# Attention scores of 96 rows as two 128-row passes and a block of four 32-row products

## The reference

```
s = (einsum('bqhd,bkhd->bhqk', qn_b, k_nope)
     + einsum('bqhr,bkr->bhqk', qr_b, k_rope)) * scale
p = softmax(s, axis=-1)
out = einsum('bhqk,bkhd->bqhd', p, v)
```

## Time and profile before

| | |
|---|---|
| median of 3 runs | 634.62 us (634.34 to 634.89) |
| profiled execution, its time | 635.12 us |
| its span in the trace | 633.3 us |
| PE / DVE / ACT / POOL busy | 99% / 69% / 56% / 50% of the span |
| PE idle before its last work | under 3 us in all |
| last matmul to the end | some 6 us |

### The profile page before, as it was taken

One profiled execution on the slowest core, in us unless ns is written; L12 is line 12 of the kernel. 1 busy time (PEld: TensorE's weight loads), 2 busy tenths in 40 slices (PEclk: granted clock), 3 DMA queues, 4 the chain that ended last, 5 costly groups with the idle time before them and its releaser, 6 DMA issues.

```text
span 633.3 us, 9322 instructions
## 1 busy us (share of the span) xinstructions
PE 624.8 (99%) x3253; PEld 525.8 (83%) x3253; DVE 439.2 (69%) x852; ACT 355.6 (56%) x765; POOL 316.4 (50%) x302
## 2 busy tenths in 40 slices
PE   8999999999999999999999999999999999999996
PEld 7889888888888887888887888888888888888885
DVE  4773335334434349999998788888888888799694
ACT  6652223213333237777776777777777778542563
POOL 3634004405656433543635776776877788610711
PEclk9999999999999999999999999999999999999999
DMA  7640026365776510100015011011010403399033
GB/s 246 198 135 1 0 84 227 127 251 164 236 263 231 185 49 1 35 1 1 10 42 175 0 43 43 1 42 28 15 43 0 142 1 135 113 344 340 0 143 124
DMA packets 41662, 66.80 MB, mean 105 GB/s; under 512 B 3496, under 2 KB 18352, under 8 KB 41488
## 3 DMA queue, kind: packets, MB, share of 16 engines
q1 hardware_dynamic: 41456, 65.95, 31.6%
q10 hardware_dynamic: 160, 0.27, 0.1%
HBM read 46.15 MB, written 20.05 MB: 105 GB/s over the span
## 4 chain that ended last, share of the span: by engine, by line
PE 94%; DVE 3%; ACT 2%; issue 1%; POOL 0%; POOLq 0%; ACTq 0%
PE ps L1429 22%; PE ps L1431 22%; PE ps L1430 22%; PE ps L1704 9%; PE ps L1722 5%; PE ps L1721 5%; PE ps L1621 2%; PE ps L1631 2%; PE ps L1632 1%; PE ps L1441 1%; PE ps L1610 1%; PE ps L1609 1%; DVE p_w L1184 1%; PE ps L1469 1%; ACT p_w L850 1%
## 5 line engine op out<-in xcount | busy, mean ns | idle before, releaser
L655 POOL TENSOR_SCALAR p_b<-p_b,stat 128x1024 f32<-128x1024 f32 x64 | 72.4, 1131 | 49.5 <-DVE stat L1283 48.8
L930 ACT ACTIVATE pT_hi<-ps 128x512 fp32r<-128x512 f32 x128 | 69.6, 596 | 45.3 <-PE ps L1704 45.3
L1288 DVE TENSOR_TENSOR pT_lo<-ps,pT_hi 128x512 fp32r<-128x512 f32 x128 | 81.8, 680 | 5.1 <-ACT pT_hi L930 5.1
L1278 DVE TENSOR_REDUCE stat<-ps 128x1 f32<-128x1024 f32 x64 | 77.7, 1214 | 10.3 <-PE ps L1431 9.8
L1429 PE MATMUL ps<-hT_hi,w_hi 128*128 128x512 f32 x208 | 83.9, 403 | 0.0
L1431 PE MATMUL ps<-hT_hi,w_lo 128*128 128x512 f32 x208 | 81.4, 391 | 0.0
L1430 PE MATMUL ps<-hT_lo,w_hi 128*128 128x512 f32 x208 | 81.1, 390 | 0.0
L919 ACT ACTIVATE p_b<-ps,stat 128x1024 f32<-128x1024 f32 x64 | 71.5, 1117 | 9.4 <-DVE stat L1278 9.3
L1704 PEld LDWEIGHTS ps<-ident,p_b 128*128 128x128 f32 x512 | 59.9, 141 | 8.9 <-issue 0.5
L1704 PE MATMUL ps<-ident,p_b 128*128 128x128 f32 x512 | 66.5, 273 | 0.1
L581 POOL TENSOR_SCALAR p_w<-p_w,stat 128x384 f32<-128x384 f32 (+1 forms) x46 | 27.1, 605 | 60.3 <-DVE stat L1199 60.3
(11 more groups left out here) (220 smaller groups left out, 1525.8 us busy)
## 6 DMA issues: line engine op xcount, KB each, us to landing
w_raw<-w_in SPq DMA_DIRECT2D x13, 512.0 KB, 4.2
x_in<-x SPq DMA_DIRECT2D x8, 512.0 KB, 3.6
wt_raw<-w_out SPq DMA_DIRECT2D x8, 512.0 KB, 4.3
t_scratch<-wt_hi SPq DMA_DIRECT2D x16, 256.0 KB, 2.4
t_scratch<-wt_lo SPq DMA_DIRECT2D x16, 256.0 KB, 2.6
wn_raw<-w_in SPq DMA_DIRECT2D x8, 336.0 KB, 3.6
q_nope_scratch<-stage SPq DMA_DIRECT2D x8, 256.0 KB, 2.4
k_nope_scratch<-stage SPq DMA_DIRECT2D x8, 256.0 KB, 2.3
```

What stands on the lines that cost most here:

```text
L655: nc.gpsimd.tensor_scalar(p_b[:, (U + 1) % 4, :], p_b[:, (U + 1) % 4, :], r_b[:, U % 4:U % 4 + 1], 0.5, ALU.mult, ALU.mult).then_inc(s_bp, 1)
L930: nc.scalar.activation(pT_hi[:, 1 - G % 2, 4 * a:4 * a + 4, U % 4 * P:(U % 4 + 1) * P], ps[:, 4 + a, :].rearrange("p (k c) -> p k c", c=P) ...
L1278: nc.vector.tensor_reduce(nm_b[:, U % 4:U % 4 + 1], ps[:, b:b + 2, :].rearrange("p b c -> p (b c)"), AX.X, ALU.max, negate=True).then_inc( ...
L1288: nc.vector.tensor_tensor(pT_lo[at_], ps[:, 4 + a, :].rearrange("p (k c) -> p k c", c=P), f(pT_hi[at_]), ALU.subtract).then_inc(s_bTl, 1)
```

## The change

The 96 rows leave 32 of the array's 128 rows unused in each of the three passes. The change fills them. The tiles of a head are laid out anew:

| tile | rows 0-63 | rows 64-95 | rows 96-127 |
|---|---|---|---|
| `q_1` | lo of nope | lo of rope | hi of rope |
| `k_1` | hi of nope | hi of rope | hi of rope |
| `q_2` | hi of nope | hi of nope (64-127) | |
| `k_2` | lo of nope | hi of nope (64-127) | |

`q_1·k_1` and `q_2·k_2` hold all but hi of q's rope times lo of k's rope. That last term has 32 rows. For two units and two halves of keys it is four products of 32 rows, each in rows of its own of `q_c` and `k_c` and into a bank of its own (`rope_b`). So two units take 8 matmuls of 128 rows and 4 of 32 rows, in place of 12 of 96 rows. `rope_b` runs once for each even unit, opens the banks of the odd unit and closes those of the even one, and so waits for the exponentials of unit U - 1.

Rows that stand twice are made by DMA copies within SBUF, eight for each head (`copy_rows` on SP: one for `q_1`, two for `q_2`, four for `q_c`, one for `k_2`), 1.125 MB in all. The first scores of a head wait for them (`s_dup`).

The loops of PE, ACT and DVE for this stage go over pairs of units, in a new order. The small edits: `k_c` is made by POOL in step 13 of the windowed attention, and `load_qk(0)` waits for it; the load of v is issued behind `copy_rows(0)`; ACT's copy of v's hi part goes from before the first exponential to behind the second; the load of `g_fin` goes to behind two loads of x; and in the opening ACT and PE take a few steps in another order, with 18 idle transposes (`spin`) in place of 16.

```
+            def copy_rows(h):
+                hp = h % 2
+                if h == 0:
+                    sp.wait_ge(s_h0, 1)
+                else:
+                    sp.wait_ge(s_sph, 2 * h - 1)
+                sp.dma_start(f(q_1[QK:P, hp, :]), f(q_h[HD:QK, :])).then_inc(s_dup, 16)
+                for i in range(2):
+                    sp.dma_start(f(q_2[i * HD:(i + 1) * HD, hp, :]), f(q_h[0:HD, :])).then_inc(s_dup, 16)
+                for i in range(4):
+                    tiles = f(q_h[HD:QK, :]).rearrange("p (a b c) -> p a b c", b=2, c=P)[:, :, i // 2, :]
+                    sp.dma_start(f(q_c[hp][i * ROPE:(i + 1) * ROPE, :]).rearrange("p (a c) -> p a c", c=P),
+                                 tiles).then_inc(s_dup, 16)
+                if h == 0:
+                    sp.wait_ge(s_h0, 2)
+                else:
+                    sp.wait_ge(s_sph, 2 * h)
+                sp.dma_start(f(k_2[HD:P, hp, :]), f(k_1[0:HD, hp, :])).then_inc(s_dup, 16)
...
+            sp.wait_ge(s_kc, 1)
             load_qk(0)
+            copy_rows(0)
+            sp.dma_start(f(k_1[HD:P, 1, :]), f(k_1[HD:P, 0, :])).then_inc(s_k1c, 16)
             sp.wait_ge(s_ws, REP * W_UNITS)
             sp.dma_start(v_raw[:, :, :], v_scr.rearrange("(t p) c -> p t c", p=P)).then_inc(s_vr, 16)
             for h in range(1, HEADS):
                 load_qk(h)
+                copy_rows(h)
...
+                if s == 13:
+                    pool.wait_ge(s_kci, 64)
+                    split(kc_raw[:, :], kc_hi[:, :], k_c[:, :], s_kch, 1, s_kc)
...
+            for U in range(0, B_UNITS, 2):
+                if U >= 10 and (U - 10) % 4 == 0:
+                    o_b_lo((U - 10) // 4)
+                if U >= 2:
+                    pT_b_hi(U - 2, 0)
+                exp_b(U)
+                if U >= 2:
+                    pT_b_hi(U - 2, 1)
+                    pT_b_hi(U - 1, 0)
+                exp_b(U + 1)
+                if U >= 2:
+                    pT_b_hi(U - 1, 1)
...
+            for U in range(0, B_UNITS, 2):
+                max_b(U)
+                if U >= 2:
+                    pT_b_lo(U - 2, 0)
+                max_b(U + 1)
+                recip_b(U)
+                if U >= 2:
+                    pT_b_lo(U - 2, 1)
+                    pT_b_lo(U - 1, 0)
+                if U >= 10 and (U - 10) % 4 == 0:
+                    o_b_sum((U - 10) // 4)
+                recip_b(U + 1)
+                if U >= 2:
+                    pT_b_lo(U - 1, 1)
...
+            def full_b(U):
...
+                    pe.wait_ge(s_dup, 128 * (h + 1))
                 if U >= 2:
                     pe.wait_ge(s_be, U - 1)
+                q, even = slice(t * P, (t + 1) * P), U % 2 == 0
+                for c in range(2):
+                    nc.tensor.matmul(ps[:, 2 * (U % 2) + c, :], q_1[:, hp, q], k_1[:, hp, c * HALF:(c + 1) * HALF],
+                                     start=even, stop=False)
...
+                for c in range(2):
+                    last = nc.tensor.matmul(ps[:, 2 * (U % 2) + c, :], q_2[:, hp, q],
+                                            k_2[:, hp, c * HALF:(c + 1) * HALF], start=False, stop=not even)
...
+            def rope_b(U):
+
+                t, hp = U % NT, U // NT % 2
+                if U >= 2:
+                    pe.wait_ge(s_be, U)
+                for i in range(4):
+                    r = slice(i * ROPE, (i + 1) * ROPE)
+                    last = nc.tensor.matmul(ps[:, i, :], q_c[hp][r, t // 2 * P:(t // 2 + 1) * P], k_c[r, :],
+                                            start=(i >= 2), stop=(i < 2))
                 last.then_inc(s_bs, 1)
...
+            for U in range(2, B_UNITS, 2):
+                beside_b = BESIDE_B.get(U, ((),) * 4)
+                gated_last(beside_b[0])
+                full_b(U)
+                rope_b(U)
+                gated_last(beside_b[1])
+                turn_b(U - 2, 0)
+                full_b(U + 1)
+                gated_last(beside_b[2])
+                turn_b(U - 2, 1)
+                if U >= 6:
+                    pv_b((U - 6) // 4, (U - 6) % 4)
+                gated_last(beside_b[3])
+                turn_b(U - 1, 0)
+                if U >= 6:
+                    pv_b((U - 5) // 4, (U - 5) % 4)
+                turn_b(U - 1, 1)
```

More of the change, by code:

```diff
@@ L148, in encoder @@
         pT_lo = at("pT_lo", 33, [P, 2, NT, HALF], F32R)
[L149 to L152, removed]
+        q_1 = at("q_1", 65, [P, 2, SEQ], F32R)
+        q_2 = at("q_2", 73, [P, 2, SEQ], F32R)
+        k_1 = at("k_1", 81, [P, 2, SEQ], F32R)
+        k_2 = at("k_2", 89, [P, 2, SEQ], F32R)
+        q_c = [at(f"q_c{i}", kb, [P, HALF], F32R) for i, kb in enumerate((140.5, 201))]
+        k_c = at("k_c", 205, [P, HALF], F32R)
+        q_h = at("q_h", 142.5, [QK, SEQ], F32R)
+        kc_raw = at("kc_raw", 115, [P, HALF])
+        kc_hi = at("kc_hi", 117, [P, HALF], F32R)
         v_raw = at("v_raw", 97, [P, NT, HEADS * HD])
@@ L353, in _ @@
             load_wn(0)
+            load_wn(1)
             load_x(1)
-            load_wn(1)
             load_wn(2)
@@ L952, in _ @@
                     nc.scalar.activation(vB[:, 1, :, 0:HD], v_raw[:, :, 0:HD], ACT.Copy).then_inc(s_sph2, 1)
-                if 2 <= U < B_UNITS + 2:
+                if U == 4:
+                    evac_g(2 * NM - 1)
+                if U == B_UNITS - 8:
+                    act.wait_ge(s_wy, W_UNITS)
+                    act.wait_ge(s_bs, B_UNITS - NT)
+                    a_hi(P1, 0, A11)
+                    a_hi(P1, 1, A11)
+                if U in (B_UNITS - 6, B_UNITS - 4):
+                    a_hi(P1, (U - (B_UNITS - 6)) // 2 + 2, A11)
+            for U in range(B_UNITS, B_UNITS + 7):
+                if U < B_UNITS + 2:
                     pT_b_hi(U - 2, 0)
                     pT_b_hi(U - 2, 1)
[L956 to L965, removed]
+                if (U - 9) % 4 == 0:
                     o_b_lo((U - 9) // 4)
@@ L1314, in _ @@
                                             ALU.subtract).then_inc(s_sp2, 1)
-                if 2 <= U < B_UNITS + 2:
+                if U == 8:
+                    evac_g(2 * NM - 1)
+            for U in range(B_UNITS, B_UNITS + 7):
+                if U < B_UNITS + 2:
                     pT_b_lo(U - 2, 0)
                     pT_b_lo(U - 2, 1)
-                if U == 8:
-                    evac_g(2 * NM - 1)
-                if U >= 9 and (U - 9) % 4 == 0:
+                if (U - 9) % 4 == 0:
                     o_b_sum((U - 9) // 4)
@@ L1691, in _, with turn_b @@
             pe.wait_ge(s_wm, REP * W_UNITS)
-            scores_b(0)
-            scores_b(1)
-            def turn_b(U):
-                pe.wait_ge(s_bp, U + 1)
-                for a in range(2):
-                    if U >= 1:
-                        pe.wait_ge(s_bTl, 2 * (U - 1) + a + 1)
-                    else:
-                        pe.wait_ge(s_wTl, W_FIRST[W_UNITS])
-                    for k in range(4):
-                        last = nc.tensor.transpose(ps[:, 4 + a, k * P:(k + 1) * P],
-                                                   p_b[:, (U + 1) % 4, (4 * a + k) * P:(4 * a + k + 1) * P], ident[:, :])
-                    last.then_inc(s_bT, 1)
+            full_b(0)
+            rope_b(0)
+            full_b(1)
+            def turn_b(U, a):
+                if a == 0:
+                    pe.wait_ge(s_bp, U + 1)
+                if U >= 1:
+                    pe.wait_ge(s_bTl, 2 * (U - 1) + a + 1)
+                else:
+                    pe.wait_ge(s_wTl, W_FIRST[W_UNITS])
+                for k in range(4):
+                    last = nc.tensor.transpose(ps[:, 4 + a, k * P:(k + 1) * P],
+                                               p_b[:, (U + 1) % 4, (4 * a + k) * P:(4 * a + k + 1) * P], ident[:, :])
+                last.then_inc(s_bT, 1)
             def pv_b(G, part):
```

95 lines of the change are left out of this document (41 added, 54 removed).

## The result

The changed kernel takes 637.00 us (median of 10 runs, 635.11 to 637.93), the one before 634.66 (10 runs, 634.34 to 634.89): a ratio of 1.0032 (of the means), interval 1.0024 to 1.0041. It is slower by 0.3%, where 0.6% faster was forecast; the time is inside the range. Two points matter for reading the profile. And after's runs spread over 2.8 us, before's over 0.6. Each run's mean granted clock is on record too, and the spread goes with it: the four runs at 0.993 or more took 635.11 to 636.37 us, the six at 0.989 to 0.992 took 636.89 to 637.93. The difference of the mean clocks, 0.0024, is over 635 us, as an estimate, 1.5 of the 1.7 us between the mean times; the trace shows one of the four, so where the six lose it isn't seen.

A forecast was written before the change was run, and what follows sets the result against it. PE's own work was taken as the bound. Head 0's copies +3.5, first units +0.8 and the stage -8.1 gave -3.8 us, 635.1 to 631.3 profiled; the median, 0.5 lower, was 630.8 us, range 627 to 642.

The forecast's parts named there:

- the copies of head 0: Before the first scores: PE waits for all eight copies and starts 3.5 us late, between 2.5 and 5.
- the rings: Dense stage: dependency loops over ACT and DVE (5.86 to 5.95 us) and over PE (5.9) make a pair 6.09.
- The block: Scores of two units: the four 32-row products cost 0.40 us, with bounds of 0.23 and 0.93.
- rival 2: Four 32-row products: weight loads go one by one, 0.53 us, 6.16 us per pair, 633.0 us; chance 0.10.
- Rival 3: Four 32-row products: array empties going in and out, 0.72 us, 6.35 per pair, 638.8 us; chance 0.16.
- two more entries of 0.08: Transposes in fours: four entries into large matmuls per two units instead of two, 0.08 us each.
- Rival 5: Dense stage: ring over ACT and DVE 0.3 us longer, 6.39 per pair, 638.9 us; chance 0.10.
- The first eight units: Units 0 to 7: late loads of v and head 1 make them 24.7 us instead of 23.9; cost 0.8, 0 to 3.
- the low clock: PE's wait at 341 us: granted clock might fall to the 1.2 GHz level, 2 us at most, in the range.
- the copies of heads 1 to 7: Dense stage: they land within some 8 us, a head lasts 24, cover is four units; cost nothing.
- step 13: Windowed attention: POOL's split of `k_c` takes 2 us, `load_qk(0)` keeps 3 us of cover; cost nothing.
- The opening: Start of the kernel: same six projection pieces by 18.3 us; 0, at most 0.5 us either way.

The follow-up runs named there:

- e6_wide_block: Changed kernel with the block's four products over all 128 rows instead of 32 each; 644.92 us, single run.
- e10_two_blocks: Changed kernel with each block of four 32-row products made twice in a row; 642.50 us, single run.
- e5_no_block: Changed kernel without the four 32-row products of each pair of units; 624.86 us, single run.
- e1_v_first: Changed kernel with the load of v issued ahead of head 0's copies; 634.36 us, ratio to the kernel before 0.9992.
- e8_v_warm: Changed kernel with v's load ahead of the copies and 44 idle transposes in PE's wait for them; 631.75 us, ratio to the kernel before 0.9953.
- e2_warm: Changed kernel with 44 idle transposes on PE while it waits for head 0's copies; 637.98 us, ratio to the kernel before 1.0047.
- e3_gate_first: Changed kernel with the last gate projection's 24 matmuls moved ahead of the first scores, into PE's wait; 636.90 us, ratio to the kernel before 1.0030.
- e7_v_gate: Changed kernel with v's load ahead of the copies and the last gate projection ahead of the first scores; 631.47 us, ratio to the kernel before 0.9952.
- e4_open_only: Kernel before with only the opening's new order on ACT and PE, without the swapped loads; 635.15 us, ratio to the kernel before 1.0007.
- e9_v_gate_split: e7_v_gate with two of the eight gate pieces put back beside unit 2; 631.81 us, ratio to the kernel before 0.9948.

## Why the prediction was wrong, point by point

**Where the 6.2 us lie.** Forecast were 630.8 us, measured 637.0. At unit 62 of the profiled execution after is 0.2 us behind before instead of 3.8 ahead, 4.0 off: 1.1 for the copies of head 0, 3.4 for units 0 to 7, -0.5 for the stage. Another 2.4 come from the median, which I put 0.5 below the profiled execution, as in the kernel before, and which is 1.9 above it; the end of the kernel gives 0.2 back. The time lies inside the range only because the range had room for rivals of another kind; neither of my two signs of being wrong (a block over 0.6 us, waits over 0.3 us in each pair) came.

**The time of a pair: the number right, its working wrong.** Laid out were 6.0 us of work for PE, drawn out to 6.09 by the rings; measured were 6.07 with the rings no part of it. The block was taken at 0.40 and costs 0.54, in size rival 2's 0.53, though its four products do start together. Rival 3's price for going in and out (0.16 and 0.16; measured 0.10 and 0.21) was right in the sum, and the 0.17 that I had put beside it for weight loads is not found on top. Against that I charged two more entries of 0.08 for splitting the transposes. They are there, but four transposes in a group take 0.35 us, and two groups with their entries 0.86, where the earlier trace rows give 0.87 for eight in one: the split costs nothing, and e6_wide_block says the same. In the pair shown above, sixteen transposes take 1.46 us (once 0.41, three times 0.35), not 1.58: with four entries 3.70 + 1.46 + 0.32 + 0.54 = 6.02, where the sum was 6.00. Two errors, +0.14 for the block and -0.12 for the transposes, cancelled; and 0.09 for rings that didn't hold stood where 0.05 of PE's 6.07 have no term. That the sum came out is luck.

The Trainium skill, page "TensorEngine Tiling (Array Packing)", Key Properties, says that a change of tiling mode drains the engine. The trace agrees, as far as gaps show it: 0.10 us ahead and 0.21 behind the block with the change of form, none in e6_wide_block without it, and one payment for two blocks in e10_two_blocks.

The Trainium skill, page "TensorE: Matmul & The Clock Gate", Part 3, gives 3.07 times for four row tiles. In this stream the block costs 0.54 us for what takes 0.92 in e6_wide_block, 1.7 times; a second block in a row costs 0.23, 4 times. The trace has both sides of that figure, and which one a kernel sees depends on how many such products stand together.

**The rings: right as a danger, too long as laid out.** I had them at 5.9 to 6.0 us; e5_no_block measures 5.72. (The ring over ACT and DVE, laid out at 5.86 to 5.95, has no block in it, so leaving the block out does not shorten it.) After is bound by PE, with a single wait of 0.21 us in the stage behind 367.3. The short waits for `pT_lo` in every pair that I expected are only in e5_no_block. Rival 5 did not come.

**The copies of head 0: the mechanism right, the size off.** The forecast was 3.5 us, between 2.5 and 5; PE waited 5.2 and began 4.6 later than before. The step that failed is SP's time for an issue: 0.50 us from loads of weights, but 0.64 from start to start for these copies, one of 1.17, so 5.8 us for eight instead of 4.0. They began 0.7 us earlier than forecast (336.86 for 337.6), which hides part of that. Landing was as read: PE starts 3.05 us behind the end of the last issue, 3.65 behind its start.

**The first eight units: the step that made the forecast wrong.** I priced them at +0.8 us, 0 to 3; measured +4.2 in the profiled execution, and more in the median. The text had the chain, in the right order: v behind the copies, head 1's loads behind v, POOL's split with unit 1's probabilities behind it. But it gave v's load the 8.5 us of the earlier trace rows, taken at a quiet time, and put head 1's loads 1 to 2 us behind it. v took 12.2, with the copies ahead of it and head 1's loads behind (DMA share 0.89 and 0.99), landed at 355.5 instead of 351, and head 1's loads at 357.1 instead of 352 to 353. With v first, units 0 to 7 take 26.8 us instead of 28.1 (e1_v_first), so the late loads are worth 1.2 us in that execution and 2.6 in the medians; with the clock up as well they take 24.5 (e8_v_warm), and 24.7 is what I had laid out. So of the +4.2 the larger part, 2.3 us, is the low clock, which the layout didn't have.

**The low clock: named, priced in the range, left out of the sum.** I wrote "if it fell, 2 us at most". By the windows it was at the 1.2 GHz level until about 351.2 (0.50, then 0.88); PE worked through 5.5 us of that, half of which is 2.8 us, and e8_v_warm against e1_v_first gives 2.6 in the medians. A wait that I forecast myself at 3.5 us, where the earlier trace rows show none over 1.5, should have had it as a term.

**Two chains side by side.** In after, the late and slow start of PE and the late loads end at nearly the same place, so the sum of the parts is not the whole. Against after's median: +1.0 (e2_warm), -0.1 (e3_gate_first) and -2.6 us (e1_v_first) alone, -5.5 together (e7_v_gate). My working added start and first units as if each had one price.

**Right at nothing:** the copies of heads 1 to 7, the weights of the output projection behind `copy_rows(7)`, and step 13. PE has no wait for them in the list above. The opening was put at 0; its edits on ACT and PE alone are within the noise (e4_open_only), and after's windowed attention ends 0.7 us earlier.

What remains of the start in e7_v_gate is 369.82 - 364.97 = 4.9 us against before; the stage gives 172.51 - 164.10 = 8.4, and unit 62 starts 3.5 us earlier than before (533.92).

## What to carry to other kernels

When a change puts transfers ahead of the first use of something, write down the whole queue that they stand in, and price what comes behind them with the transfers around it, not with a duration from a quiet time; large loads with no tie to them go first. A wait of several us at the head of a stage costs more than itself if the granted clock falls behind it (in e7_v_gate it fell behind one of 1.45 us), so fill it or keep PE busy, and if that alone gives nothing, look for a second chain that ends at the same place before dropping it. Small-row products gain by standing together: the price of 0.31 us is for the change of form, not for the product. And when runs of one kernel spread, look at each run's mean clock before taking the profiled one for all of them.

## What the runs showed of the hardware

- Going into and out of the 32-row form costs 0.10 and 0.21 us in a stream of 128-row matmuls, once per change (e6_wide_block, e10_two_blocks). At both places the weight loads start with their matmuls and not some 0.2 us ahead.
- Four 32-row products of 512 columns in four row groups start within about 0.02 us of one another; a second block of four behind the first takes one slot of 0.23 us.
- A copy inside SBUF keeps SP for 0.60 us and 0.64 from start to start (one took 1.17, and one alone at 365.00 took 0.51); 256 KB land in a median of 3.0 to 3.4 us, 64 KB in 2.8, 128 KB in 2.3. So the small ones are not the quickest; the 64 KB copies take every other 128 columns of their source, the others whole rows. After's groups of DMA issues (count, KB each, median us to landing):

```profile
q<-q_h SPq DMA_DIRECT2D x16, 256.0 KB, 3.4
...
k<-k SPq DMA_DIRECT2D x9, 256.0 KB, 3.0
...
q_c<-q_h SPq DMA_DIRECT2D x32, 64.0 KB, 2.8
v_raw<-v_scratch SPq DMA_DIRECT2D x1, 2048.0 KB, 12.2
...
q<-q_h SPq DMA_DIRECT2D x8, 128.0 KB, 2.3
```

- After 5.2 us without a matmul the granted clock was at the 1.2 GHz level from 345 to about 351 us, where two passes took up to 1.0 us instead of 0.55. It fell as well behind waits of 3.1 us (e2_warm), 5.4 us (e3_gate_first) and 1.45 us (e7_v_gate), and not behind the wait of 0.97 us that ends at 367.3 in after, nor behind one of 1.4 us in e9_v_gate_split. With 44 idle transposes, 4.96 us, in the wait for the copies it was 1.00 there and in the first units (e2_warm, e8_v_warm), so here transposes held it up as other matmuls do.
